# Gathering the expert rows of a token inside the last two expert blocks, in order of their row numbers

## What is computed

```
grp = argmax(xn2 @ w_rg + b_rg)                        # one of 4 groups
top_v, top_i = top_k(e_logits[grp], 2)                 # two of its 8 experts
top_w = softmax(top_v) * p_grp
y[token] = x[token] + sum over its two choices of top_w * expert(xn2[token])
expert(x) = (silu(x @ w_gate) * (x @ w_up)) @ w_down   # 1024 -> 512 -> 1024
```

## Time and profile before

| | |
|---|---|
| median of 3 runs | 1593.61 us (1592.26 to 1596.3) |
| the profiled execution | 1597.38 us, of which the span is 1595.6 us |
| PE, DVE, ACT, POOL busy | 91%, 62%, 46%, 13% of the span |
| moved by DMA | 347.56 MB, mean 218 GB/s |
| expert stage | about 950 to 1551 us of the span |
| combine stage | about 1552 us to the end |

### The profile page before, as it was taken

How to read it: one execution, slowest core, us unless ns; L and a number is a source line. 1 busy time by engine, 2 the same in 40 slices (tenths; PEclk the granted TensorE clock), 3 DMA queues, 4 the chain that set the end, 5 groups by cost and what they waited for, 6 DMA issues and landing times. The chain is left out here.

```text
span 1595.6 us, 22136 instructions
## 1 busy us (share of the span) xinstructions
PE 1459.4 (91%) x8287; PEld 1250.7 (78%) x8287; DVE 986.9 (62%) x1316; ACT 737.7 (46%) x869; POOL 201.2 (13%) x233
## 2 busy tenths in 40 slices
PE   5999999989999999899899939999999999999960
PEld 5999999979999999789788726777777777777740
DVE  4422321136565555767656566888888888888845
ACT  6421121134444444332312116777777777777732
POOL 2600000011111110200100012111111111111004
PEclk8999999989999999999999959999999999999985
DMA  6222227243333321667641058999999999999818
GB/s 223 76 75 75 75 75 248 90 148 98 98 97 97 97 90 58 172 174 238 229 169 57 28 226 280 399 387 394 386 394 395 399 389 394 397 395 394 311 56 331
DMA packets 135558, 347.56 MB, mean 218 GB/s; under 512 B 13529, under 2 KB 91805, under 8 KB 109825
## 3 DMA queue, kind: packets, MB, share of 16 engines
q1 hardware_dynamic: 125224, 312.11, 54.0%
q0 software_dynamic: 6160, 21.89, 4.4%
q10 hardware_dynamic: 4120, 12.85, 2.0%
HBM read 292.91 MB, written 54.89 MB: 218 GB/s over the span
## 5 line engine op out<-in xcount | busy, mean ns | idle before, releaser
L2090 DVE TENSOR_TENSOR e_w_lo<-mixed,e_w_hi 128x2048 fp32r<-128x2048 f32 x64 | 145.7, 2296 | 11.6 <-ACT e_w_hi L2022 11.6
L2090 DVE TENSOR_TENSOR e_w_lo<-w_out,e_w_hi 128x2048 fp32r<-128x2048 f32 x64 | 143.4, 2282 | 0.0
L2022 ACT CAST e_w_hi<-mixed 128x2048 fp32r<-128x2048 f32 x64 | 120.3, 1906 | 37.6 <-PEq L94 21.2
L884 PE MATMUL gate_banks<-f_hi,wg_hi 128*128 128x360 f32 (+1 forms) x368 | 124.3, 338 | 1.9 <-PEq L94 1.5
L2022 ACT CAST e_w_hi<-w_out 128x2048 fp32r<-128x2048 f32 x64 | 121.8, 1902 | 1.7 <-PE e_up L2160 1.7
L885 PE MATMUL gate_banks<-f_lo,wg_hi 128*128 128x360 f32 (+1 forms) x368 | 121.0, 329 | 0.0
L886 PE MATMUL gate_banks<-f_hi,wg_lo 128*128 128x360 f32 (+1 forms) x368 | 120.9, 329 | 0.0
L1997 POOL CAST e_idx<-token_of_slot 96x1 uint32 (+1 forms) x33 | 51.9, 1573 | 460.7 <-PE e_x L2147 425.9
L2158 PE MATMUL e_gate<-e_w_hi,e_x_hi 128*96 128x512 f32 x256 | 104.0, 406 | 3.3 <-DVE e_x_lo L2094 1.9
L2180 PE MATMUL e_y<-e_w_hi,e_hT_hi 128*96 128x512 f32 x256 | 103.7, 405 | 3.4 <-DVE e_w_lo L2090 3.4
L2181 PE MATMUL e_y<-e_w_lo,e_hT_hi 128*96 128x512 f32 x256 | 102.1, 399 | 0.0
(11 more groups left out here) (510 smaller groups left out, 3542.5 us busy)
## 6 DMA issues: line engine op xcount, KB each, us to landing
w_out<-in_w_down_e SPq DMA_DIRECT2D x64, 1024.0 KB, 9.1
mixed<-in_w_gate_e SPq DMA_DIRECT2D x32, 1024.0 KB, 8.4
mixed<-in_w_up_e SPq DMA_DIRECT2D x32, 1024.0 KB, 9.3
w_gate<-in_w_gate_e SPq DMA_DIRECT2D x32, 1024.0 KB, 8.4
w_up<-in_w_up_e SPq DMA_DIRECT2D x32, 1024.0 KB, 9.2
expert_rows<-e_y_rows ACTq DMA_DIRECT2D x32, 384.0 KB, 7.5
proj<-mixed SPq DMA_DIRECT2D x8, 1408.0 KB, 6.1
proj_tile<-proj SPq DMA_DIRECT2D x8, 1408.0 KB, 6.2
```

Of the source, the lines that this page charges most:

```text
L884: pe.matmul(bank, wg_hi[j][:, k, :], hi, start=(k == 0), stop=False)
L2022: act.copy(hi(i, step, j), raw(i, u, j)).then_inc(hi_ready[i], 1)
L2090: dve.tensor_tensor(lo(i, u, j), raw(i, u, j), hi(i, step, j).bitcast(F32), ALU.subtract).then_inc(lo_ready[i], 1)
```

## The change

It has five parts.
1. In `project` the zero fill covers blocks 30 and 31 too (24 blocks for 22).
2. In `route` POOL clears `R.weight`, and DVE copies one column (`R.extra_blocks`).
3. In `experts`, behind DVE's part of block 1, DVE runs `choices_in_order` once: 19 small operations on values of 128x18, 128x9 or 128x1; 13 of them are linked, which means that DVE waits on a semaphore for the result before it goes on. For each token the choice with the lower row number becomes "first", the other "second", and the weights are swapped with them. Row numbers of the second from block 30 on are "late": `row_of[1]` gets 65536 added for them, `row_of[2]` for all the others, so that each of the two gathers skips the rows of the other.
4. At the end of `experts` POOL issues two sets of nine gathers. The first set (second choices outside the last two blocks, into the buffers of gate and up weights of u = 0) waits for the stores of blocks 28 and 29 and for up(30). The second set (all first choices, into the buffers of u = 1) waits for the store of block 30 and for up(31). ACT issues the store of block 30 only when the first set has landed, and the store of block 31 only when the second set has landed. DVE adds the first choices, weighted, to `R.x2`, behind its last split.
5. In `combine` POOL issues nine gathers of the late rows over the first set's tiles; DVE adds the second choices to `R.x2` in one operation for each tile; SP stores `R.x2`. The 18 gathers, ACT's nine scalings and DVE's other nine additions are gone from it.

```diff
 # project, SP
-                spare = a["expert_rows"][NE * SLOTS:MAXB * SLOTS, :].rearrange("(b s) d -> s b d", s=SLOTS)
+                spare = a["expert_rows"][(NE - 2) * SLOTS:MAXB * SLOTS, :].rearrange("(b s) d -> s b d", s=SLOTS)
...
-                    sp.dma_start(spare[:, :, i * D // 2:(i + 1) * D // 2], bc(zeros[:], 1, MAXB - NE)).then_inc(spare_filled, 16)
+                    sp.dma_start(spare[:, :, i * D // 2:(i + 1) * D // 2], bc(zeros[:], 1, MAXB - NE + 2)).then_inc(spare_filled, 16)
 # route
+                pool.memset(R.weight[:], 0.0)
+                dve.tensor_copy(R.extra_blocks[:], incl[:, NE - 1:NE])
 # experts, buffers
+        wide = lambda u: [nc.alloc_sbuf_tensor_at(f"rows{u}{i}", [P, 4, D], F32, offset=R.w_at[u][i]) for i in range(2)]
+        halves = [wide(1), wide(0)]
+        R.rows = [[halves[n][t // 4][:, t % 4, :] for t in range(NT)] + [xb[1 - n][:TS, :]] for n in range(2)]
 # experts, POOL, behind its last gather of tokens
+                pool.wait_ge(s["rows_known"], 1)
+                for u in range(2):
+                    pool.wait_ge(stored[u], 16 * more)
+                    pool.sem_inc(s["idx_seen"], 1)
+                for t in range(NR):
+                    if t == NT:
+                        pool.wait_ge(s["xT_full"], 2 * more + 3)
+                    else:
+                        pool.wait_ge(done[UP], 4 * more + 2)
+                    r = tile_rows(t)
+                    pool.sem_inc(s["idx_seen"], 1)
+                    pool.indirect_dma_start(R.rows[1][t][:r], None, a["expert_rows"], bass.IndirectOffsetOnAxis(ap=R.row_of[1][:r, t:t + 1], axis=0),
+                                            bounds_check=MAXB * SLOTS - 1, oob_is_err=False).then_inc(R.rows_loaded[1][t], 16)
+                pool.wait_ge(stored[0], 16 * more + 16)
+                pool.sem_inc(s["idx_seen"], 1)
+                pool.wait_ge(stored[1], 16 * more)
+                pool.sem_inc(s["idx_seen"], 1)
+                pool.wait_ge(done[UP], 4 * more + 4)
...
+                for t in range(NR):
+                    r = tile_rows(t)
+                    pool.indirect_dma_start(R.rows[0][t][:r], None, a["expert_rows"], bass.IndirectOffsetOnAxis(ap=R.row_of[0][:r, t:t + 1], axis=0)).then_inc(R.rows_loaded[0][t], 16)
 # experts, ACT
-                def down_out(b, u, tt):
+                def down_out(b, u, tt, gathered=None):
...
                     act.wait_ge(s["y_act"], b + 1)
+                    if gathered is not None:
+                        act.sem_inc(s["idx_seen"], 1)
+                        for t in range(NT + 1):
+                            act.wait_ge(R.rows_loaded[gathered][t], 16)
                     act.dma_start(a["expert_rows"][bass.ds(b * SLOTS, SLOTS), :], yb[u][:]).then_inc(stored[u], 16)
...
-                down_out(end - 1, 0, more)
+                down_out(end - 1, 0, more, 1)
...
-                down_out(end, 1, more)
+                down_out(end, 1, more, 0)
 # experts, DVE
+                def choices_in_order():
+                    own = Own(dve, s["order_own"])
+                    L = own.link
+                    w = [R.weight[:, :, j] for j in range(2)]
+                    low_row, high_row, swap, w0, w1 = scratch[:5]
+                    L(dve.tensor_copy(dest_two[:], R.dest[:]))
+                    d = [dest_two[:, j * NR:(j + 1) * NR] for j in range(2)]
+                    dve.tensor_tensor(low_row[:], d[0], d[1], ALU.min)
+                    dve.tensor_tensor(high_row[:], d[0], d[1], ALU.max)
+                    L(dve.tensor_tensor(swap[:], d[0], d[1], ALU.is_gt))
...
+                    L(dve.tensor_copy(R.row_of[0][:], low_row[:]))
+                    late, limit = scratch[5], scratch[6][:, 0:1]
...
+                    L(dve.tensor_scalar(late[:], high_row[:], limit, None, ALU.is_gt))
+                    L(dve.scalar_tensor_tensor(R.row_of[1][:], late[:], 65536.0, high_row[:], ALU.mult, ALU.add))
...
+                    dve.sem_inc(s["rows_known"], 1)
                 step(1, 1)
+                choices_in_order()
                 with dve.Fori(1, more + 1) as tt:
...
+                for t in range(NR):
+                    r = tile_rows(t)
+                    dve.wait_ge(R.rows_loaded[0][t], 16)
+                    dve.scalar_tensor_tensor(R.x2[:r, t, :], R.rows[0][t][:r], R.weight[:r, t, 0:1], R.x2[:r, t, :], ALU.mult, ALU.add).then_inc(R.x2_ready, 1)
 # combine
-                pool.tensor_copy(idx[:], R.dest[:]).then_inc(idx_ready, 1)
-                pool.wait_ge(idx_ready, 1)
...
-                        pool.indirect_dma_start(rows[j][t][:r], None, a["expert_rows"], bass.IndirectOffsetOnAxis(ap=idx[:r, i:i + 1], axis=0)).then_inc(loaded[t], 16)
...
+                    pool.wait_ge(R.rows_loaded[1][t], 16)
+                    pool.indirect_dma_start(R.rows[1][t][:r], None, a["expert_rows"], bass.IndirectOffsetOnAxis(ap=R.row_of[2][:r, t:t + 1], axis=0),
+                                            bounds_check=MAXB * SLOTS - 1, oob_is_err=False).then_inc(R.rows_loaded[1][t], 16)
...
-                    act.activation(rows[0][t][:r], rows[0][t][:r], ACT.Copy, scale=R.weight[:r, t, 0:1]).then_inc(first, 1)
...
-                    dve.scalar_tensor_tensor(rows[0][t][:r], rows[1][t][:r], R.weight[:r, t, 1:2], rows[0][t][:r], ALU.mult, ALU.add).then_inc(added, 1)
-                    dve.wait_ge(added, 2 * t + 1)
-                    dve.tensor_tensor(rows[0][t][:r], rows[0][t][:r], R.x2[:r, t, :], ALU.add).then_inc(added, 1)
+                    dve.wait_ge(R.rows_loaded[1][t], 32)
+                    dve.scalar_tensor_tensor(R.x2[:r, t, :], R.rows[1][t][:r], R.weight[:r, t, 1:2], R.x2[:r, t, :], ALU.mult, ALU.add).then_inc(added, 1)
```

More of the change, by code:

```diff
@@ L1927, in experts @@
         low = [[nc.alloc_sbuf_tensor_at(f"e_w_lo{u}{i}", [P, PIECE * 2], F32R, offset=R.w_at[u][i]) for i in range(3)] for u in range(2)]
+        NR = NT + 1
+        scratch, dest_two = [sb(f"scratch{i}", [P, NR]) for i in range(7)], sb("dest_two", [P, 2 * NR])
         h_hi, h_lo = (sb(f"hT_{n}", [P, KF, SLOTS], F32R) for n in ("hi", "lo"))
@@ L1931, in experts @@
         names = """idx_ready idx_seen all_stored xT_full x_hi_ready x_lo_ready silu_ready h_ready hT_full h_hi_ready h_lo_ready
-            y_act""".split()
+            y_act order_own rows_known""".split()
         s = {n: sem("e_" + n) for n in names}
@@ L2125, in _ @@
                 x_split(1, 1)
+                def choices_in_order():
[8 more added lines that the diff above has]
+                    L(dve.tensor_tensor(swap[:], d[0], d[1], ALU.is_gt))
+                    dve.tensor_tensor(w0[:], w[0], swap[:], ALU.mult)
+                    L(dve.tensor_tensor(w1[:], w[1], swap[:], ALU.mult))
+                    dve.tensor_tensor(w[0], w[0], w0[:], ALU.subtract)
+                    L(dve.tensor_tensor(w[1], w[1], w1[:], ALU.subtract))
+                    dve.tensor_tensor(w[0], w[0], w1[:], ALU.add)
+                    dve.tensor_tensor(w[1], w[1], w0[:], ALU.add)
+                    L(dve.tensor_copy(R.row_of[0][:], low_row[:]))
+                    late, limit = scratch[5], scratch[6][:, 0:1]
+                    L(dve.tensor_scalar(limit, R.extra_blocks[:], 0.5, (NE - 1) * 0.5 - 0.25, ALU.mult, ALU.add))
+                    L(dve.tensor_scalar(limit, limit, 1.5 * 2.0 ** 23, None, ALU.add))
+                    L(dve.tensor_scalar(limit, limit, -1.5 * 2.0 ** 23, None, ALU.add))
+                    L(dve.tensor_scalar(limit, limit, 2.0 * SLOTS, -0.5, ALU.mult, ALU.add))
+                    L(dve.tensor_scalar(late[:], high_row[:], limit, None, ALU.is_gt))
+                    L(dve.scalar_tensor_tensor(R.row_of[1][:], late[:], 65536.0, high_row[:], ALU.mult, ALU.add))
+                    L(dve.tensor_scalar(high_row[:], high_row[:], 65536.0, None, ALU.add))
+                    L(dve.scalar_tensor_tensor(R.row_of[2][:], late[:], -65536.0, high_row[:], ALU.mult, ALU.add))
+                    dve.sem_inc(s["rows_known"], 1)
                 step(1, 1)
+                choices_in_order()
                 with dve.Fori(1, more + 1) as tt:
@@ L2212, in combine @@
         sem = ctx.enter_context(stage_semaphores(nc))
-        sb = lambda n, s, dt=F32: ctx.enter_context(nc.sbuf_tensor("c_" + n, s, dt))
         NR = NT + 1
[L2215 to L2220, removed]
+        stored, added = sem("c_stored"), sem("c_added")
         with nc.Block() as block:
@@ L2224, in _ @@
             def _(pool):
[L2225 to L2226 removed]
                 for t in range(NR):
                     r = tile_rows(t)
[L2229 to L2234 removed]
+                    pool.wait_ge(R.rows_loaded[1][t], 16)
+                    pool.indirect_dma_start(R.rows[1][t][:r], None, a["expert_rows"], bass.IndirectOffsetOnAxis(ap=R.row_of[2][:r, t:t + 1], axis=0),
+                                            bounds_check=MAXB * SLOTS - 1, oob_is_err=False).then_inc(R.rows_loaded[1][t], 16)
+            @block.vector
```

(12 more changed lines are left out.)

## The result

The changed kernel takes 1601.74 us (median of 7 runs, 1598.21 to 1602.64), the kernel before 1594.18 us in the runs beside it (7 runs, 1592.26 to 1596.3). The ratio is 1.0036 with a 95% interval of [1.0023, 1.0049]: slower by 0.36%, where 0.25% less was forecast. The time lies 0.7 us above the range of 1579 to 1601 us, and the sign is the one to which the prediction gave a chance of 0.15.

A forecast was written before the change was run, and what follows sets the result against it. In combine the DMA engines are full and PE idle, so gathers were moved ahead of it. The sum -8.9 + 3.2 + 0.1 + 1.6 = -4.0 took the median 1593.61 to 1589.6 us, range 1579 to 1601.

The forecast's parts named there:

- Zero fill: Start of the kernel: two more zeroed blocks delay the wg load, ACT's copies and so PE, by 3.2 us.
- Choices: Expert stage: choices_in_order takes DVE 3.1 us and stalls PE 1.6 us as gate(2) begins, bounds 1.3 and 2.5.
- The start together: What the change adds ahead of the end stage: zero fill 3.2, route copy 0.1 and ordering the choices 1.6 us.
- The end stage: End of experts through combine: moving most gathers ahead ends the span at 1586.7 for 1595.6 us, saving 8.9.
- the landing of the last gather of each set: End of experts: the last gather lands 4 us after its start in the first set, 4.3 being the least seen.
- The wait ahead of store 30: End of experts: ACT held from 1529.63 to 1540, down(31) 7.2 us late, said to cost nothing by itself.
- d: Extra time per POOL issue from the bounds check; 18 issues on the chain, slower by over 0.3% from 0.49 us.
- the slower rival: POOL's gathers: the bounds check makes each of 18 issues dearer, 1607.6 us at 1 us each; chance 0.13.
- POOL's issues do not keep DVE out: Combine: denies the rival that POOL and DVE take turns, 22.7 us for late tiles against 16.2, 1596.1; chance 0.03.
- rival 1: POOL's gathers: issues not held by DVE or cheap where rows are skipped, 1.24 us throughout, 1580 us; chance 0.14.
- rival 2: Start and expert stage: the additions ahead of the end are hidden, net -8.9, 1584.7 us; chance 0.08.
- Skipped rows are not moved into SBUF: Combine: denies the rival that skipped rows are moved, late gathers bringing 4.45 MB again, near 1594 us; chance 0.04.

The follow-up runs named there:

- wg_first_before: The kernel before with SP's load of wg ahead of the zero fill: 1593.41 us against 1595.44, ratio 0.9987.
- zero24_before: The kernel before with only the change's zero fill (24 blocks for 22), plus the block count assertion: 1599.68 us against 1595.44, ratio 1.0024.
- the base: The changed kernel with the bounds of the block count asserted at run time: 1599.69 us, ratio 1.0029 to the kernel before.
- casts_first: The changed kernel, with the assertion, with ACT's casts for block 31 moved ahead of the held store of block 30: 1598.49 us.

## Why the prediction was wrong

The sign came out wrong through sizes of terms, most of them in the end stage. The mechanisms of the steps held, with one left out: PE's lower clock behind the longer wait.

1. **Zero fill**, forecast 3.2. The slower of the two transfers lands 44.0 us after its issue for 41.0, and the wait grew by 2.98 us (1.40 to 4.38), as worked out. What the step left out is that the longer wait drops PE to the lower clock level for the matmuls behind it, 2.1 us. Measured alone: 4.2 us.
2. **Choices**, forecast 1.6. The operations took 3.1 us (994.13 to 997.22) as reckoned; PE waited 1.82. By the medians 2.3, within the bounds given (1.3 to 2.5). A term that the sum did not have lies behind it: each turn of the loop takes 36.05 us for 35.99, in every run with the changed expert stage, with the choices early or late. From store 1 to store 29 that is 0.9 us. Its cause stays open.
3. **The start together**, forecast 4.9, was 7.05 in the profiled execution (1519.60 - 1512.55); 4.2 + 2.3 = 6.5 by the runs. The 7.05 is in part chance. Store 0 to store 29 is 2.95 of it, and 6.8 was there at the end of the projection (322.78 for 315.98). But 1.7 of these 6.8 lie ahead of the zero fill (its first transfer is issued at 246.69 for 244.99), and 2.7 came off again in the stages between, which the change hardly touches: they took 674.7 us in this execution of the kernel before, 672.0 in the changed kernel's, and 672.1 and 673.0 in the traces of `wg_first_before` and `zero24_before`.
4. **The end stage**, forecast -8.9, was -1.95 in the changed kernel's execution and -3.65 in the base's. This is the step that failed. The term with the largest error is the landing of the last gather of each set: 4.0 and 4.3 us in the sum, 5.9 and 7.1 measured, 4.7 us of the 7.0 that are missing. It was set at the value of a gather alone. The late gathers are 1.2 us short, landing again for the greater part, and POOL's way to its first issue in combine 0.7.
5. **The wait ahead of store 30** was in the sum: the second set starts 3.3 us behind the held store there, 4.1 measured. "It costs nothing by itself" was said of down(31), and casts_first bears that out (1.2 us at most). So this wait does not explain the miss. What the prediction never did was to price the change without it; the run without the hold shows 8.5 us, as much as the whole gain that was forecast for the end stage. It is the dearest thing that the change brings with it, ahead of the zero fill; taking away either of the two turns the loss into a small gain.
6. **Rivals.** Issues with skipped rows take 0.99 us for 0.94, d = 0.05: the slower rival did not happen, though its sign did. POOL's issues do not keep DVE out (the additions run at 1.28 us beside them). DVE's hold on issues held everywhere, so rival 1 is out, and PE did wait for both additions ahead, so rival 2 is too. Skipped rows are not moved into SBUF: late gathers landed in 2.8 to 5.3 us, and POOL's queue moved as many bytes as before, though 27 gathers name 1088 rows more than 18 do.
7. **The range.** 1579 to 1601 left out the value by 0.7 us. Errors of one sign in a chain of seven terms add, and the range had only the bounds of single unknowns. In the profiled executions the forecast is 9.1 us off (7.0 at the end, 2.15 ahead of it); in the medians 11.6, since the execution of the kernel before that was profiled lay 3.2 us above its median and the changed kernel's 0.9.

For the last point of 6, the queue of POOL's transfers (packets, MB, share) and the sums of HBM traffic, first of the kernel before, then of the changed one:

```profile
q0 software_dynamic: 6160, 21.89, 4.4%
...
HBM read 292.91 MB, written 54.89 MB: 218 GB/s over the span
```

```profile
q0 software_dynamic: 7392, 21.90, 4.7%
...
HBM read 297.37 MB, written 55.68 MB: 221 GB/s over the span
```

## What to carry to other kernels

Price each wait that a change adds by what is behind it on every engine, the waiting instruction's own transfer included: here a store held for a gather of other rows put a second set of gathers 8.5 us later (first issue 33.55 us behind store 29 for 25.04). Where new work is cut into sets, take the landing of each set's last transfer under the set's own traffic, not alone, and count the way from that landing to the next issue. And a transfer added to a queue far from the change can be dear: two more blocks of zeros ahead of a small load cost 4.2 us, nearly all that the base of these runs lost (4.6), and loading it first gives that back and 2 us more.

## What the runs showed of the hardware

- After waits of 4.38 us (the base) and 4.22 us (`zero24_before`) PE's granted clock read 0.55 and 0.50 in the window of 295 to 300 us, with PE busy throughout; with the wait of 1.40 us it stayed at 1.00. By the 14 matmuls lost, such a wait cost half as much again as it lasted.
- An indirect DMA with a bounds check takes POOL 0.99 us to issue, whether a few of its rows or nearly all are skipped, and one without 0.94. With nearly all skipped the first of a set lands in 2.96 us in the changed kernel, against 4.3 for one of 512 KB alone.
- Each skipped row still leaves a trace. The changed kernel has 1088 skipped rows; POOL's queue has 1232 packets more for 0.01 MB, and the profile's sum of HBM reads is 4.46 MB higher, just the size of 1088 rows of 4 KB. It is so in every run with a bounds check and in none without. Whether these rows are read from HBM and dropped, or only counted, no run here shows.
- A gather's issue that starts beside a DVE instruction with two operands in SBUF ends 0.8 to 0.9 us after that instruction. The Trainium skill ("SBUF — State Buffer", who interferes with whom) says that such a DVE instruction contends with a GpSimd instruction that reads SBUF; the trace agrees, with 2.85 us for the issue at 1532.82 in the changed kernel, and with 0.95 us for the first two issues once DVE's pair was moved away.
